# A third second-level Strassen product per pair in two feed-forward layers of a one-core kernel

## The reference

```python
# first model, twice (layers 0 and 1 here, the "plain" ones)
def swiglu(x, w1, w3, w2):
    return (silu(x @ w1) * (x @ w3)) @ w2

# second model, twice (layers 2 and 3 here, the "convolved" ones)
def conv_ffn(h, w_up, conv_w, conv_b, w_down):
    up = h @ w_up
    up = conv1d(up, conv_w, causal, width 3, per channel) + conv_b
    val, gate = split(up, 2)
    return (silu(gate) * val) @ w_down
```

## Time and profile before

| | |
|---|---|
| median of 3 runs | 2668.95 us (2668.88 to 2674.04) |
| profiled execution | 2669.95 us, of which span 2668.2 us |
| TensorE busy (share of span) | 2578.8 us (97%) |
| VectorE, GpSimd, ScalarE busy | 1681.1 us (63%), 1232.2 us (46%), 595.9 us (22%) |
| mean granted TensorE clock | 0.983 |
| layer 0, up part | from 19.8 to 288.2 us of the span |
| layer 1, up part | from 829.0 to 1096.2 us |

### The profile page before, as it was taken

The page is one execution under the profiler, slowest core; times in us unless marked ns, Lnnn a source line. Parts: engine busy times, 40 slices in busy tenths (PEclk is TensorE's granted clock), DMA queues, the critical chain, the costliest instruction groups (busy, mean ns, idle before and its releaser), DMA issues.

```text
span 2668.2 us, 33470 instructions
## 1 busy us (share of the span) xinstructions
PE 2578.8 (97%) x12942; PEld 2056.1 (77%) x12942; DVE 1681.1 (63%) x2859; ACT 595.9 (22%) x1172; POOL 1232.2 (46%) x1128
## 2 busy tenths in 40 slices
PE   7999999999999999999999989999999699999999
PEld 6999889888467889886654567999644567899888
DVE  6776512588656887523498765677652875788721
ACT  2111001432201111002235642222202621222200
POOL 6666532440435677440000254677031884677642
PEclk9999999999999999999999999999999799999999
DMA  6555422221124555421122012223330422122222
GB/s 205 182 189 170 158 87 79 95 64 64 48 71 139 175 166 181 156 89 53 48 63 79 17 32 72 75 91 104 105 86 11 148 91 79 64 95 95 91 78 68
DMA packets 244062, 264.26 MB, mean 99 GB/s; under 512 B 31744, under 2 KB 226112, under 8 KB 243776
## 3 DMA queue, kind: packets, MB, share of 16 engines
q1 hardware_dynamic: 227968, 206.89, 24.5%
q10 hardware_dynamic: 15936, 55.22, 5.9%
HBM read 255.14 MB, written 6.29 MB: 98 GB/s over the span
## 4 chain that ended last, share of the span: by engine, by line
PE 88%; DVE 6%; POOL 2%; issue 2%; ACT 1%; DMA 0%; SPq 0%; DVEq 0%; ACTq 0%
PE ps L791 27%; PE ps L836 14%; PE ps L746 9%; PE ps L1615 6%; PE ps L589 6%; PE ps L2203 5%; PE ps L1434 3%; PE ps L3213 3%; PE ps L2238 2%; PE ps L1588 1%; PE ps L1744 1%; PE ps L1575 1%; POOL phase L3469 1%; PE ps L1158 1%; PE ps L2251 1%
## 5 line engine op out<-in xcount | busy, mean ns | idle before, releaser
L791 PE MATMUL ps<-hT,ring 128*128 128x256 f32 x2176 | 505.0, 381 | 7.9 <-DVE phase L1013 4.7
L791 PEld LDWEIGHTS ps<-hT,ring 128*128 128x128 f32 x2176 | 411.2, 191 | 67.5 <-issue 9.1
L624 POOL TENSOR_TENSOR ring<-ring 128x512 f32<-128x512 f32 (+1 forms) x124 | 168.7, 1360 | 552.5 <-DMA ring<-in_ffn_w 301.1
L836 PE MATMUL ps<-phase,ring 128*128 128x256 f32 x1848 | 400.1, 379 | 1.6 <-DVE phase L945 1.5
L836 PEld LDWEIGHTS ps<-phase,ring 128*128 128x128 f32 x1848 | 351.2, 190 | 50.0 <-DVE phase L945 2.3
L791 PE MATMUL ps<-phase,ring 128*128 128x256 f32 x1472 | 349.2, 381 | 6.2 <-DVE act_t L856 5.5
L791 PEld LDWEIGHTS ps<-phase,ring 128*128 128x128 f32 x1472 | 274.5, 191 | 41.6 <-DVE act_t L856 6.7
L627 POOL TENSOR_TENSOR ring<-ring 128x512 f32<-128x512 f32 (+2 forms) x204 | 237.6, 1165 | 0.0
L2561 POOL TENSOR_SCALAR phase<-phase 128x128 f32<-128x128 f32 (+3 forms) x64 | 33.4, 535 | 334.9 <-DVE phase L2530 334.9
L626 POOL TENSOR_TENSOR ring<-ring 128x512 f32<-128x512 f32 (+1 forms) x124 | 167.7, 1353 | 9.7
L629 POOL TENSOR_TENSOR ring<-ring 128x512 f32<-128x512 f32 (+1 forms) x124 | 171.1, 1380 | 0.0
(11 more groups left out here) (451 smaller groups left out, 4403.5 us busy)
## 6 DMA issues: line engine op xcount, KB each, us to landing
ring<-in_ffn_w SPq DMA_DIRECT2D x60, 1024.0 KB, 5.4
phase<-in_ada_w ACTq DMA_DIRECT2D x96, 512.0 KB, 3.5
ring<-in_ffn_w_up SPq DMA_DIRECT2D x44, 1024.0 KB, 5.0
ring<-in_w_in SPq DMA_DIRECT2D x19, 1024.0 KB, 5.2
ring<-in_attn_w_in SPq DMA_DIRECT2D x14, 1024.0 KB, 5.2
ring<-in_ffn_w_down SPq DMA_DIRECT2D x8, 1408.0 KB, 6.3
ring<-in_ssm_w_glu SPq DMA_DIRECT2D x8, 1024.0 KB, 5.7
ring<-in_ffn_w_down SPq DMA_DIRECT2D x8, 1024.0 KB, 5.1
```

Of the source, the lines that this page charges most:

```text
L624: pool.tensor_tensor(s1, a21, a22, ALU.add).then_inc(combined, 1)
L791: mm = pe.matmul(ps[:, 4 * w + bank_of[name], 0:HALF], left[:, c], right[name](c), start=(opens and c == 0), stop=(c == KC // 2 - 1), skip ...
L836: mm = pe.matmul(ps[:, bank_of[name], 0:HALF], left[:, r - lo], right(name, r), start=(half == 0 and r == 0), stop=(r == NP - 1), skip_gro ...
```

## The change

In the plain layers a third inner product, w = 4, takes P4 of both slots. It uses the weight blocks that P4 used and the token sum t4 of the first level. The new order there for p >= 1 is: (0,P1), (1,P1), opening of 2, opening of 3, (0,P5), (0,P2), closing of 2, (1,P5), (1,P2), closing of 3, opening of 4, (0,P3), (1,P3), closing of 4. VectorE has 25 steps: 17 to 21 take in the opening of 4, 22 and 23 the P3, 24 and 25 the closing of 4. The layer's slots are free after (4,P3). GpSimd makes the weight sums of w = 4 and, in pair 1, its token sums too. The second SiLU part and the second product come behind steps 24 and 25.

In pair 0 of the plain layers two slabs are left in place of four, the inner token sums go between the steps of w = 1, and g_mix of pair 0 goes behind pair 1; six slabs a layer are left to the down part. In all layers TensorE waits for the inner token sums one kind at a time (t1, t2, t3, t4), and P1 of the down part waits for the gated values only, P6 for the token sums. In the convolved layers t4 moves behind the last step of w = 1. The taps keep their order; their code is only cut into single tiles. The steps of the rotary table go behind eight pairs, one each, in place of four.

```diff
-    order = [(0, "P1"), (1, "P1")] + [(w, name) for w in INNER for name in ("P1", "P6", "P7", "P5")]
-    order += [(0, "P5"), (0, "P2")] + [(2, name) for name in ("P2", "P4", "P3")] + [(1, "P5")]
-    order += [(3, name) for name in ("P2", "P4", "P3")]
-    return order + [(1, "P2"), (0, "P4"), (0, "P3"), (1, "P4"), (1, "P3")]
+    opening, closing = ("P1", "P6", "P7", "P5"), ("P2", "P4", "P3")
+    order = [(0, "P1"), (1, "P1")] + [(w, name) for w in (2, 3) for name in opening]
+    order += [(0, "P5"), (0, "P2")] + [(2, name) for name in closing] + [(1, "P5")]
+    if 4 not in INNER[k]:
+        order += [(3, name) for name in closing] + [(1, "P2")]
+        return order + [(w, name) for w in range(2) for name in ("P4", "P3")]
+    order += [(1, "P2")] + [(3, name) for name in closing] + [(4, name) for name in opening]
+    return order + [(0, "P3"), (1, "P3")] + [(4, name) for name in closing]
...
-                put(n + 2 * b + w, e + EVENTS[k]["up", b, w, "P3"])
+                put(n + 2 * b + w, e + EVENTS[k]["up", b, 4 if b and 4 in INNER[k] else w, "P3"])
...
+        def h_inner_last_pool(pool, k):
+
+            b11, b12, b21, b22 = inner_right(4)
+            t1, t2, t4 = inner_sums(k, 4)[0]
+            pool.wait_ge(h_mixed, 4 * k + 4)
+            pool.tensor_tensor(t1, b12, b11, ALU.subtract).then_inc(last_mixed, 1)
...
+            pool.wait_ge(tile_done, TILE0[f"ffn{k}"] + EVENTS[k]["up", 0, 1, "P4"])
+            pool.tensor_tensor(b12, b22, b12, ALU.subtract).then_inc(last_mixed, 1)
...
                 if name == "P1":
-                    pe.wait_ge(quad, quad_up(k, p - 1, w - 2, "P6") if p > 1 else quad_up(k, 0, 0, "P6" if w == 2 else "P4"))
+                    if w == 4:
+                        pe.wait_ge(quad, quad_pair(k, p, 9))
+                    elif p > 1:
+                        pe.wait_ge(quad, quad_pair(k, p - 1, 14 if w == 3 else 25 if 4 in INNER[k] else 9))
+                    else:
+                        pe.wait_ge(quad, quad_up(k, 0, 0, "P6" if w == 2 else "P4"))
                     pe.wait_ge(combined, combined_up(k, p, 1, w))
-                    if p == 1:
-                        pe.wait_ge(in_mixed, 8 * k + 8)
+                if p == 1 and name in ("P5", "P6", "P7", "P4"):
+                    if w == 4:
+                        pe.wait_ge(last_mixed, 4 * k + ("P5", "P6", "P4", "P7").index(name) + 1)
+                    else:
+                        pe.wait_ge(in_mixed, 8 * k + 2 * ("P5", "P6", "P7", "P4").index(name) + 2)
                 if name == "P2":
-                    pe.wait_ge(quad, quad_pair(k, p, 4 if w == 2 else 8))
+                    pe.wait_ge(quad, quad_pair(k, p, {2: 4, 3: 8, 4: 21}[w]))
...
                                 if q == 0 and name == "P1":
+                                    pe.wait_ge(gated, FC * k + 2 * r + 2)
+                                if q == 0 and name == "P6":
                                     pe.wait_ge(g_mixed, G_MIXED0[k] + 4 * (r + 1))
...
+            if step == 17:
+                dve.wait_ge(in_copied, copies + 3)
+                add(v4, v4, inner(4, 3, 4))
+            if step == 18:
+                after(17)
+                add(g[0][:, P:], g[0][:, P:], v4)
+            if step == 19:
+                x = g[1].rearrange("p (s t) -> p s t", s=2)
+                add(x, x, v4.unsqueeze(1).to_broadcast([P, 2, P]))
+            if step in (20, 21):
+                after(step - 1)
+                add(g[1][:, P:], g[1][:, P:], inner(4, 2, 3) if step == 20 else inner(4, 1, 2))
...
-        SLAB_BEHIND = (8, 9, 16)
+        SLAB_BEHIND = (8, 9, 21, 25)
...
-                    for w in range(2):
-                        for step in range(1, 6):
-                            first_step(dve, k, w, step)
-                            if step in (3, 5):
-                                ada_slab_dve(dve, k, 2 * w + (step == 5))
-                        h_inner_dve(dve, k, ("t1", "t2", "t4") if w == 0 else ("t3",))
+                    for step in range(1, 6):
+                        first_step(dve, k, 0, step)
+                        if step in (3, 5):
+                            ada_slab_dve(dve, k, step // 5)
+                    for step in range(1, 6):
+                        first_step(dve, k, 1, step)
+                        if step in (1, 2, 4):
+                            h_inner_dve(dve, k, ({1: "t1", 2: "t2", 4: "t3"}[step],))
                     product(p, 0)
+                    h_inner_dve(dve, k, ("t4",))
+                    product(p, 1)
...
-            h_inner_dve(dve, k, ("t1", "t2", "t4"))
-            earlier(0, 0)
-            for step in range(1, 6):
+            h_inner_dve(dve, k, ("t1", "t2"))
+            for i in (1, 0):
+                tile_taps(0, 0, i)
+            for step in range(1, 5):
                 first_step(dve, k, 1, step)
             h_inner_dve(dve, k, ("t3",))
+            first_step(dve, k, 1, 5)
+            h_inner_dve(dve, k, ("t4",))
```

More of the change, by code:

```diff
@@ L924, in pair_step @@
                 add(quadrants[w][:, 3 * HALF:], g[w], ps[:, 4 * w + 3, 0:HALF])
-            if step in (17, 19):
-                w = (step - 17) // 2
-                done(w, "P4")
-                add(g[w], g[w], ps[:, 4 * w, 0:HALF])
-            if step in (18, 20):
-                w = (step - 18) // 2
+            if 4 not in INNER[k]:
+                if step in (17, 19):
+                    w = (step - 17) // 2
+                    done(w, "P4")
+                    add(g[w], g[w], ps[:, 4 * w, 0:HALF])
+                if step in (18, 20):
+                    w = (step - 18) // 2
+                    done(w, "P3")
+                    add(quadrants[w][:, HALF:2 * HALF], halves[:, w, :], ps[:, 4 * w + 3, 0:HALF])
+                return
+            if step == 17:
[10 more added lines that the diff above has]
+                add(g[1][:, P:], g[1][:, P:], inner(4, 2, 3) if step == 20 else inner(4, 1, 2))
+            if step in (22, 23):
+                w = step - 22
                 done(w, "P3")
                 add(quadrants[w][:, HALF:2 * HALF], halves[:, w, :], ps[:, 4 * w + 3, 0:HALF])
+            if step == 24:
+                done(4, "P3")
+                add(g[0], g[0], inner(4, 0, 2))
+            if step == 25:
+                add(g[1][:, 0:P], g[1][:, 0:P], inner(4, 2, 3))
         def g_mix_dve(dve, k, r):
@@ L2613, in strassen_conv_act @@
                     silu(p - 1, 0)
-                    for w in INNER:
+                    for w in (2, 3):
                         inner_copy_act(act, k, p, w)
@@ L2665, in strassen_conv_dve @@
                     pair_step(dve, k, p, step)
-                earlier(p, 0)
+                for i in (1, 0):
+                    tile_taps(p, 0, i)
                 pair_step(dve, k, p, 19)
                 pair_step(dve, k, p, 20)
-            earlier(NP - 1, 1)
-            product(NP - 1, 1)
-            product(NP - 1, 0)
+            for i in (1, 0):
+                tile_taps(NP - 1, 1, i)
+            for i in (1, 0):
+                product(NP - 1, i)
             if k in STRASSEN_DOWN:
```

240 lines of the change are left out of this document (135 added, 105 removed).

## The result

The changed kernel takes **2643.96 us** (median of 4 runs, 2641.99 to 2646.21) against 2668.91 us of the kernel before in the same comparison (2666.2 to 2674.04): ratio 0.9905, 95% interval 0.9887 to 0.9922, so 21 to 30 us less. A second timing gave 2646.13 against 2670.92 us, ratio 0.9904 (0.9889 to 0.992). The forecast was 2652.5 us with a range of 2647 to 2666: the direction was right, the gain was some 8 us larger than forecast, and the range did not reach it. The profiled execution took 2643.05 us, its span is 2641.1 us.

The account below looks back on a forecast made before the run. The prediction took TensorE's matmul work to bound the plain layers, with waits in their first pairs. Terms -6.6, -11.3, -1.4, -1.3, +2.1 and +2.0 sum to -16.5: 2653.5 us profiled, 2652.5 us median, range 2647 to 2666.

Parts of the forecast that it names:

- third small product: Pairs 1 to 10 of both plain layers: two large P4 products become seven small ones, 0.33 us saved per pair, -6.6 us.
- first pairs of the plain layers: TensorE's losses of 6.4 and 4.9 us at the start of the two plain layers both go, -11.3 us.
- convolved starts: Start of the convolved layers: two of six token sums leave the way to step 2, 0.7 us twice, -1.4 us.
- down products, layer 3: Down part: P6 instead of P1 waits for the token sums, saving 1.3 of 1.5 us at L945, -1.3 us.
- what comes back in pair 2: Pair 2 of the plain layers: moved g_mix and a table step delay step 4, so (2,P2) waits, +2.1 us.
- thin slacks at (4,P2) and (0,P3): Plain pairs: slacks of 0.3 and 0.5 us before these products, charged 0.1 us a pair, +2.0 us.
- the signs: Listed trace signs of a right forecast, among them plain pairs repeating after 23.2 us and no waits at L945.
- The large sums meet steps 18 and 19: Rival, plain pairs: late slots let GpSimd's large sums delay step 21, 0.9 us wait a pair, 2668.5 us; chance 0.12.
- The waits at the start: Rival, first pairs of the plain layers: the waits only move, 11.3 us stay, 2664 us; chance 0.12.
- the bound of any later pair: Rival, plain pairs: VectorE becomes the bound at about 26 us against 23.2, kernel slower at 2676 us; chance 0.08.

Follow-up runs that it names:

- after_timed_again: The changed kernel with no edit, timed again in five rounds beside the kernel before on the same chip: 2646.13 us, ratio 0.9904.
- before_again: The kernel before with no edit, profiled a second time: 2664.05 us.

## Why the forecast fell short

Step by step, by the prediction's own terms, from the table:

| term | forecast | measured |
|---|---|---|
| third small product | -6.6 | -6.5 |
| first pairs of the plain layers | -11.3 | -10.4 and -11.1 |
| convolved starts | -1.4 | -1.6 |
| down products, layer 3 | -1.3 | -1.4 and -1.1 |
| what comes back in pair 2 | +2.1 | 0 |
| thin slacks at (4,P2) and (0,P3) | +2.0 | 0 |
| table steps in layer 1 | not seen | -2.5 and -1.9 |

- **Right: where the time was.** The four gains came to 0.1 to 0.9 us of their forecasts. The pair repeats after 23.19 us, the gaps at the end of the first pairs are closed, L856's waits are more than halved, and the experiments name the pieces: the block of token sums in layer 0, what stands ahead of the gated product in both. Of the waits at L945 0.6 us stay, where the signs said none.
- **Wrong: "What comes back".** This step failed: the wait at (2,P2) of pair 2, +2.1 us, didn't come. The step priced the extra four adds at 0.42 to 1.4 us and took about the middle of bounds 1.8 us apart, which don't follow from these prices (four adds at them lie 3.9 us apart). The prediction had in hand that GpSimd's large sums begin 5.5 to 6.5 us into a pair, and that VectorE is done with one g_mix by about 5; the term doesn't say which adds would then meet GpSimd. Measured in layer 1, GpSimd begins at 7.3 us, the adds end at 6.7 and the table step at 7.1, and step 4 ends at 877.46 - 867.86 = 9.6, due at 10.5. The run without the third product shows that the mechanism was real and its price even larger: the third product itself takes it away, by freeing the slots later. In layer 1 it does so narrowly: in after_timed_again the sums began at 6.6 us, the table step took 1.50 us beside them, and step 4 ended 0.15 us ahead of (2,P2).
- **Wrong: the +2.0 for thin slacks.** This step failed too. A slack is a margin and becomes a cost only where it is used up. The size was right at the low end (0.3 us forecast, 0.25 to 1.36 measured; steps 18 and 19 met GpSimd's small sums, as foreseen), but no pair of the three profiles of after used it up. With the two pairs found in other runs that is 0.8 + 0.2 us in eight profiles, 0.1 us a run in place of 2.0.
- **Missed: the table steps.** In before TensorE waited 2.0 us in two pairs of layer 1 behind VectorE's two table steps a pair (1.3 us in the second profile). The prediction had the diff of the steps but costed only where they go, not what they leave.
- **The rest.** These three make 6.0 to 6.6 us. With the small differences of the other terms they carry the forecast's gain of 16.5 to the 22.4 and 22.8 of the ruler. The medians say 25, twice. The ruler lies within both intervals of the runs; where the other 2 us are, no profile shows, since the untouched stages move by more than that between executions. That stays open.
- **The rivals.** The large sums meet steps 18 and 19 almost never: in pair 2 of layer 1 they end at 885.64, 17.8 us into the pair, and step 18 begins at 19.2. From pair 2 on they begin 6.1 to 9.5 us into the pair in the three profiles of after, mostly later than the 5.5 to 6.5 forecast, and reach step 18 in one pair of 60, without a wait. Where a load lands as late as 10.6 or 11.2 us, as in the two pairs above, the rival's mechanism is there: one wait of 0.55 us, for 0.9 in its sum. The waits at the start are gone and not moved. VectorE has 4 us more to do in all and was not the bound of any later pair in after. What the Trainium skill, "SBUF — State Buffer", section "Who interferes with whom", says of a VectorE instruction with two SBUF inputs beside GpSimd is borne out by the runs without the third product (1.4 to 1.5 us beside GpSimd, 0.42 apart); in pair 2 it cost TensorE a wait only where GpSimd was not held back.

## What to carry to other kernels

When an edit moves the moment at which a buffer comes free, follow it to the engine that works on the next load: here a release that came later put GpSimd's sums behind VectorE's and so removed a wait, and without it one wait instruction did the same. Charge a margin by how often it is used up, and look on both sides of a moved step: at the place it goes to and at the waits in the place it leaves. Where whole runs scatter by more than the effect, cut the span at instructions that repeat and compare the pieces.

## What was not expected of the hardware

*The same wait, with and without a slow clock behind it.* In layer 1 TensorE waits 3.3 us for the gated product in both profiles of before. The windows just behind that wait, first before, then before_again (length, busy times of PE, PEld, DVE, ACT, POOL, granted clock, DMA share, GB/s):

```profile
859.00:862.20 3.20, 3.17 (x8) 2.63 (x9) 3.13 (x3) 0.00 (x0) 2.47 (x2) 0.55 0.34 136
```

```profile
858.30:860.10 1.80, 1.76 (x8) 1.61 (x9) 1.77 (x2) 0.00 (x0) 1.13 (x1) 1.00 0.53 213
```

One execution was granted 0.55, near the lower level of 1.2 GHz, for the next product, the other full speed (2.4 GHz): 1.4 us of difference behind equal waits, and in the run with the table steps alone 2.9 us behind a wait of 3.5. A wait's price is its length plus a piece that is not the same every time.

*Stages that nobody touched.* The second mixer took 395.8 us after and 401.7 us in the run with one add more in the first pairs. The 15 us from 55 us after its start on, in that run and then after:

```profile
1267.60:1282.60 15.00, 15.00 (x54) 12.67 (x55) 0.67 (x2) 3.53 (x7) 0.00 (x0) 0.58 0.23 71
```

```profile
1266.10:1281.10 15.00, 15.00 (x57) 11.24 (x57) 1.99 (x3) 5.09 (x10) 0.00 (x0) 0.79 0.23 71
```

The granted clock is 0.58 against 0.79. Compared instruction by instruction the first run falls back by 3.0 us from 53 to 63 us after the start; the rest of the 6 us lies in similar stretches at the stage's start and near its end. One run of a kernel of this length says nothing about an effect below 5 us; the pieces above do.
